# Token decays of a hybrid GLA and gated-delta block prepared inside its input projection, with the last gate stores on SP's queue

## The reference

```python
h = modulated_rmsnorm(x)                       # context and latent tokens, same weights
p = h @ w_in                                   # q, k, v, gates, a low rank r, and a, beta per head
log_alpha = -exp(a_log) * softplus(a + dt_bias)    # per token, direction and head
beta      = sigmoid(beta_b)
# gated delta rule, both directions, chunks of 64 tokens:
g = cumsum(log_alpha, over the chunk)
A = eye + tril(beta * (k @ k.T) * exp(g_i - g_j), -1)
U, W = solve(A, beta * v), solve(A, beta * exp(g) * k)
k_dec, a_chunk = k * exp(g_last - g), exp(g_last)
# beside it gated linear attention with a decay per key dimension
y = x + gate1 * (concat(norm(o) * silu(gate)) @ w_out)
out = rmsnorm(y + gate2 * (square(relu(modulated_rmsnorm(y) @ w1)) @ w2))
```

## Time and profile before

| | us |
|---|---|
| runs, median of 3 | 1803.25 (1802.39 to 1804.13) |
| profiled execution | 1795.54 |
| its span, first to last instruction | 1793.5 |
| PE busy in the span | 1572.9 |
| mean granted clock of PE | 0.951 of full |

### The profile page before, as it was taken

How to read it: one execution, slowest core, us unless ns; L and a number is a source line. 1 busy time by engine, 2 the same in 40 slices (tenths; PEclk the granted TensorE clock), 3 DMA queues, 4 the chain that set the end, 5 groups by cost and what they waited for, 6 DMA issues and landing times. The chain is left out here.

```text
span 1793.5 us, 35173 instructions
## 1 busy us (share of the span) xinstructions
PE 1572.9 (88%) x15022; PEld 1325.9 (74%) x15022; DVE 1011.8 (56%) x1542; ACT 641.6 (36%) x976; POOL 425.6 (24%) x376
## 2 busy tenths in 40 slices
PE   4599999999966888878776798789999989899997
PEld 1366887999966777777775587568888867787876
DVE  2534553101104776777776755845545588887975
ACT  3366435221102222232222223455545543333333
POOL 1301111111112455555554311323223200000000
PEclk7799999999987998999998899899999999999999
DMA  7213424426543543333322232034453487163422
GB/s 307 75 53 97 120 69 123 133 85 197 172 121 90 151 125 100 112 113 108 108 62 66 94 126 98 24 123 136 153 170 130 156 317 256 63 235 109 173 83 94
DMA packets 169565, 229.81 MB, mean 128 GB/s; under 512 B 34189, under 2 KB 101121, under 8 KB 168386
## 3 DMA queue, kind: packets, MB, share of 16 engines
q1 hardware_dynamic: 162562, 205.79, 35.2%
q0 software_dynamic: 6848, 21.76, 3.8%
HBM read 165.78 MB, written 61.73 MB: 127 GB/s over the span
## 5 line engine op out<-in xcount | busy, mean ns | idle before, releaser
L87 PE MATMUL fps<-xh_m,w1r_hi 128*128 128x512 f32 x448 | 177.6, 396 | 18.9 <-ACT s L2321 5.4
L87 PE MATMUL fps<-bh,ah 128*128 128x512 f32 x448 | 176.4, 394 | 13.6 <-DVE acc L2636 9.1
L88 PE MATMUL fps<-xl_m,w1r_hi 128*128 128x512 f32 x448 | 176.7, 394 | 0.0
L89 PE MATMUL fps<-xh_m,w1r_lo 128*128 128x512 f32 x448 | 176.5, 394 | 0.0
L89 PE MATMUL fps<-bh,al 128*128 128x512 f32 x448 | 176.0, 393 | 0.0
L88 PE MATMUL fps<-bl,ah 128*128 128x512 f32 x448 | 175.8, 392 | 0.0
L80 PE MATMUL ps_main<-hhi,whi 128*128 128x512 f32 (+3 forms) x360 | 136.4, 379 | 15.7 <-DVE wlo L647 11.8
L82 PE MATMUL ps_main<-hhi,wlo 128*128 128x512 f32 (+3 forms) x360 | 132.8, 369 | 0.0
L81 PE MATMUL ps_main<-hlo,whi 128*128 128x512 f32 (+3 forms) x360 | 132.7, 369 | 0.0
L2283 ACT ACTIVATE ah<-araw 128x2048 fp32r<-128x2048 f32 x28 | 53.7, 1918 | 186.4 <-PE fps L89 120.7
L80 PE MATMUL ps_main<-whi,hhi 128*128 128x256 f32 x416 | 120.0, 288 | 0.0
(11 more groups left out here) (307 smaller groups left out, 3596.6 us busy)
## 6 DMA issues: line engine op xcount, KB each, us to landing
s_hid<-hb SPq DMA_DIRECT2D x112, 256.0 KB, 2.3
araw<-s_hid SPq DMA_DIRECT2D x28, 1024.0 KB, 6.6
w1raw<-in_w_ff SPq DMA_DIRECT2D x16, 1024.0 KB, 6.2
w2b<-in_w_ff SPq DMA_DIRECT2D x16, 1024.0 KB, 6.2
raw<-in_w_in SPq DMA_DIRECT2D x14, 1024.0 KB, 5.2
wa<-in_w_ada SPq DMA_DIRECT2D x8, 1024.0 KB, 10.5
z_sb<-in_w_ada SPq DMA_DIRECT2D x16, 512.0 KB, 4.5
n_sb<-in_w_ada SPq DMA_DIRECT2D x16, 512.0 KB, 4.3
```

The source lines that it names most:

```text
L87: pe.matmul(out, lhi, rhi, start=start, stop=False, skip_group_check=True)
L88: pe.matmul(out, lhi, rlo, start=False, stop=False, skip_group_check=True)
L89: return pe.matmul(out, llo, rhi, start=False, stop=stop, skip_group_check=True)
```

## The change

Running sums, exponentials, token scales and turned rows are made inside the two value units of the projection. Their three masks are loaded there, into a buffer that the low-rank decays have left (`lr_x`). POOL stores the rows to DRAM during the second value unit. Results live in the memory of `K.gt2`, which is now allocated from the start; its own row gates are made at the start of merging. In mixing, SP issues the keys and `decays(0)` first; the remaining four masks follow, each with its own wait where it is used, instead of one wait for all. The stores of the last gate unit are issued by SP instead of POOL.

The core of the diff:

```diff
@@ project_phase, SP
+            def load_sums():
+                for b in range(2):
+                    sp.wait_ge(st_lr[b], 80)
+                for x, n in enumerate(("k_tri", "k_trix", "k_chunk")):
+                    sp.dma_start(sum_m[:, x], A[n]).then_inc(ld_sums, 16)
+            def store_gate(t):
+                sp.wait_ge(main_out, out_by[(LAST_GATE, "gate", t)])
+                nt = NSTORES - TL + t
+                sp.dma_start(S["gate"][t, :, 3 * W:4 * W], t_sb[:, nt % 4]).then_inc(st_g[t % 4], 16)
             for u in range(NU):
                 load_unit(u)
+                if u == VA - 1:
+                    load_sums()
...
             for g in range(10, NLATE):
                 load_late(g)
+                if g - 4 >= NLATE - TL:
+                    store_gate(g - 4 - NLATE + TL)
+            for t in range(TL - 4, TL):
+                store_gate(t)
+            for i in range(4):
+                sp.wait_ge(st_g[i], 32)
@@ project_phase, POOL
+                        if u == LAST_GATE:
+                            continue
+                        if (u, t) == (VA + 1, 6):
+                            pool.wait_ge(row_out, 1)
+                            pool.dma_start(S["row"].rearrange("x r n -> r x n"),
+                                           rowt.rearrange("r (x n) -> r x n", x=3)).then_inc(st_row, 16)
@@ project_phase, ACT: copy and exponentials after tile 3 of the first value unit, rows after tile 3 of the second
+                    if (u, j) == (VA, 3):
+                        act.wait_ge(g_ready, 1)
+                        act.activation(K.gcol, sums(0), ACT.Copy).then_inc(sm_act, 1)
+                        act.activation(K.sm[:, :, :, 2], sums(1), ACT.Exp).then_inc(sm_act, 1)
+                        act.activation(K.egc, sums(0), ACT.Exp).then_inc(sm_act, 1)
+                        act.activation(K.aB.rearrange("p c d t h -> p (c d t h)"), ps_tr[:, 0, 160:320], ACT.Exp).then_inc(sm_act, 1)
+                    if (u, j) == (VA + 1, 3):
+                        act.wait_ge(row_ready, 1)
+                        act.activation(rowt, ps_tr[:80, 1, :3 * P], ACT.Copy).then_inc(row_out, 1)
@@ project_phase, DVE: token_scales() at tile 6 of the first value unit, the 24 operations of lines 1271 to 1281
@@ project_phase, PE
+            def running_sums():
+                pe.wait_ge(ld_sums, 48)
+                pe.wait_ge(ab_kept, 2)
+                pe.wait_ge(tr_out, NTR * 8)
...              (the six products of lines 1453 and 1455)
+            def turn_rows():
+                pe.wait_ge(sm_act, 4)
...              (the three transposes of line 1469)
+                    if (u, j) == (VA, 0):
+                        running_sums()
+                    if (u, j) == (VA + 1, 0):
+                        turn_rows()
@@ mix_phase, SP
-            for dst, n in ((tri, "k_tri"), (trix, "k_trix"), (chunk, "k_chunk"), (lev_m, "k_lev"), (inc_m, "k_inc"),
-                           (eye, "k_eye"), (smask, "k_smask")):
-                sp.dma_start(dst[:], A[n]).then_inc(ld_mask, 16)
             keys(0)
+            decays(0)
+            constants(ld_lev, (lev_m, "k_lev"), (eye, "k_eye"))
+            constants(ld_tri, (tri, "k_tri"))
             linear(0)
             values(0)
             token_keys(0)
-            sp.wait_ge(rt_out, 1)
-            sp.dma_start(S["row"].rearrange("x r n -> r x n"), rowt[:]).then_inc(st_row, 16)
-            sp.wait_ge(st_row, 16)
-            decays(0)
+            constants(ld_inc, (inc_m, "k_inc"))
+            constants(ld_sel, (smask, "k_smask"))
@@ mix_phase, POOL
-            pool.wait_ge(ld_mask, 16 * N_MASK)
-            pool.wait_ge(sm_dve, 3)
             differ(0)
@@ mix_phase, ACT
+            act.preload_act_table_set("natural_log_exp_and_others")
-            for x in range(4):
+            for x in range(2):
@@ mix_phase, waits added in every step (DVE first_inverse and accumulate, PE first_inverse and cumulate)
+                dve.wait_ge(ld_lev, 32)
+                dve.wait_ge(ld_sel, 16)
+                    pe.wait_ge(ld_lev, 32)
+                pe.wait_ge(ld_tri, 16)
@@ mix_phase, PE: rows(2), rows(3), the sums and the turns are gone
@@ merge_phase, ACT and PE
+            for x in range(2):
+                act.wait_ge(rows_done, x + 1)
+                act.activation(K.gt2[:, x * 512:(x + 1) * 512], ps_p[:, x], ACT.Copy).then_inc(row_out, 1)
+            for x in range(2):
+                for i in range(4):
+                    last = pe.matmul(ps_p[:, x, i * P:(i + 1) * P], K.mod[:, 40 + 4 * x + i, 0:1].broadcast_to([P, P]), K.ident[:],
+                                     start=True, stop=True)
+                last.then_inc(rows_done, 1)
             inter(0)
```

More of the change, by code:

```diff
@@ L362, in project_phase @@
         ar_ready, ar_out, sel_done = m.sem("ar_ready"), m.sem("ar_out"), m.sem("sel_done")
+        ld_sums, ab_kept, g_ready = m.sem("ld_sums"), m.sem("ab_kept"), m.sem("pg_ready")
+        sm_act, sm_dve, row_ready, row_out, st_row = (
+            m.sem("psm_act"), m.sem("psm_dve"), m.sem("row_ready"), m.sem("row_out"), m.sem("st_row"))
+        st_g = [m.sem(f"st_g{i}") for i in range(4)]
+        VA = [un[0] for un in UNITS].index("va")
+        LAST_GATE = NU - 1
+        sum_m = lr_x[:].rearrange("p a n -> p (a n)")[:, :6 * P].rearrange("p (x d n) -> p x d n", x=3, d=2)
+        rowt = lr_e[:80, :3 * P]
         outs = []
@@ L623, in _ @@
                 else:
-                    if nt >= 4:
+                    if u == LAST_GATE and j >= 4:
+                        act.wait_ge(st_g[j % 4], 16)
+                    elif nt >= 4:
                         act.wait_ge(st_t[nt % 4], 16 * (nt // 4))
@@ L726, in _, with token_scales @@
             for t in range(NT):
-                dve.tensor_copy(K.beta[:, :, pos_of(t), :], zc[:, t, :].rearrange("p (z h) -> p z h", z=2))
+                last = dve.tensor_copy(K.beta[:, :, pos_of(t), :], zc[:, t, :].rearrange("p (z h) -> p z h", z=2))
+            last.then_inc(ab_kept, 1)
+            def token_scales():
+                half = lambda c: slice(c * C, (c + 1) * C)
+                dve.wait_ge(ab_kept, 2)
+                dve.wait_ge(sm_act, 4)
+                dve.tensor_copy(K.sm[:, :, :, 1], K.beta[:]).then_inc(sm_dve, 1)
+                dve.scalar_tensor_tensor(K.sm[:, :, :, 0], K.egc, -1.0, K.beta[:], ALU.mult, ALU.mult).then_inc(sm_dve, 1)
+                dve.wait_ge(sm_dve, 2)
+                for n in range(2):
+                    dve.tensor_copy(K.smn[half(n), n], K.sm[half(n), 0])
+                    for s in range(NT):
+                        back = 11 - s if s >= TC else 1 - s
+                        dve.tensor_copy(K.smn[half(1 - n), n, s], K.sm[half(1 - n), 1, back])
             for i, (u, kind, j, s) in enumerate(outs):
@@ L1529, in predict @@
                     after(pe, st_done[d], 2 * s + n)
-                if s == 0 and n == 0:
-                    pe.wait_ge(row_out, 4)
                 for h in range(NH):
@@ L1539, in query @@
                 pe.wait_ge(qd_done, s - TC + 1)
+                if s == TC and n == 0:
+                    pe.wait_ge(row_out, 2)
                 for d in R2:
@@ L2813, in hybrid_block @@
         K.beta = m.sb("beta", [P, 2, NT, NH])
+        K.gt2 = m.sb("gt2", [P, D])
+        K.sm, K.smn = (K.gt2[:, 240 * x:240 * (x + 1)].rearrange("p (d t z h) -> p d t z h", d=2, t=NT, z=3) for x in range(2))
+        K.gcol, K.egc = (K.gt2[:, 480 + 80 * x:560 + 80 * x].rearrange("p (d t h) -> p d t h", d=2, t=NT) for x in range(2))
+        K.aB = K.gt2[:, 640:800].rearrange("p (c d t h) -> p c d t h", c=2, d=2, t=NT)
         with ExitStack() as ctx_h:
```

94 lines of the change are left out of this document (33 added, 61 removed).

## The result

The kernel with the change took 1783.03 us, the median of 4 runs from 1780.32 to 1786.23, against 1802.99 us for the kernel before run beside it (4 runs, 1802.39 to 1804.13). The ratio is 0.9889 with a 95% interval of 0.9871 to 0.9908: faster by 16.6 to 23.3 us, with 20.0 in the middle. The forecast was -18.0 us, 1785.3. In four later series of runs the kernel before took 1795.2 to 1799.8 us at the median, so some of these 20 us may be chance; the repeat further down gives 16.4.

What follows compares the result with a forecast made beforehand. PE bounds the value units, a chain of waits the time from 523 to 559 us. Terms -5.3 - 15.2 + 2.0 + 0.5 + 0 = -18.0 us take 1803.25 to 1785.3, range 1780.5 to 1792.5.

Steps and rivals of the forecast that it cites:

- Stores on SP: End of projection: SP issues the last gate unit's stores, POOL's 5.045 us drain is hidden, release 523.4 not 528.7; gain 5.3 us.
- The rule of the Trainium skill that was weighed: Projection's end: issuing from another engine saves only issue time, about 0.28 us; the total would be -13.0 instead of -18.0.
- Prologue: Start of mixing: POOL's first product 8.3 us after the phase begins instead of 23.5; gain 15.2 us, keys' delay taken as nothing.
- `gla`: Mixing's start: decay operand could be late, ready at 15.4 against an inverse due at 14.1; taken as nothing, up to 1.3 lost.
- PE waiting for `gla`: Sign of being wrong: at mixing's start PE stands waiting for the decay operand's load.
- Value units: Projection's value units: PE takes up six products and three turned columns; loss 2.0 us, between 1.6 and 3.3.
- The four changes between kinds of matmul: PE in the projection's value units: one more instruction's 0.11 us for each change, an estimate.
- Added waits: Every mixing step: DVE gets 10 + 32 more semaphore waits, PE 20 + 10; loss 0.5 us, between 0 and 2.4.
- Gate rows: Start of merging: sixteen matmuls moved there while PE idles; taken as nothing, between a loss of 0.6 and a gain of 1.3.
- the longer head: Rival, mixing's start: keys and decay operand cost 1.5 and 1.3 us, waits 2.4; -13.3, 1790.0 us; chance 0.12.
- The drain stayed: Rival, projection's end: POOL's 5 us settle only when the phase ends, gain 0.3 instead of 5.3; 1790.3 us; chance 0.11.
- the last stage's clock: Rival: PE gets a lower clock after shorter rest; under about 0.945 eats 18 us, at 0.93 gives 1813; chance 0.03.

## Why the prediction was right, point by point

*Stores on SP.* Forecast -5.3, between 4.9 and 5.6; measured -5.6 in the trace. The drain fell under the last gate unit, and SP's own, forecast at the 0.37 us of the earlier trace rows, took 7 ns. That the drain "is paid on POOL's list whenever it comes" is shown by the run in which it was paid 27 us late. That it belongs to the stores that POOL issued fits its 50 to 54 ns for each transfer. The rule of the Trainium skill that was weighed (DMA: Bandwidth & Descriptors, section Issuing engines are not separate DMA queues) would have left this part at 0.3 us; here the trace does not agree, with 5.6 us, as the issuing engine also decides whose list, and whose drain, comes last. What stays open is why stores on SP alone gained nothing in the timings.

*Prologue.* Forecast a head of 8.3 us instead of 23.49; measured 8.19 and 8.41. The keys ahead of the spreading loads cost what the sum held for them and no more: with the order turned the head is 7.35, shorter by 0.85 us, which is their issue.

*`gla`.* This step failed, and "PE waiting for `gla`" was one of the signs of being wrong that I had named. I took nothing, as "Its queue is much emptier than in the row", with 1.3 us as the bound. It landed 5.8 us after its issue at 534.70, as in the earlier trace rows, and cost 1.60 us against before; in the other profiles 0.3 to 1.1 (6.08 to 6.90 less 5.81). Its queue was not emptier: by the sizes of SP's issues ahead of it some 1.6 MB stood there in both kernels, as the eight small loads (512 KB) took the place of masks. The bound had the right working and was 0.3 us too low; choosing its good end had no row behind it.

*Value units.* Forecast +2.0, measured +1.65. The sums came to 1.34 against 1.26 and the turns to 0.31 against 0.37. The four changes between kinds of matmul, put at 0.11 each, were not there.

*Added waits.* Forecast +0.5, measured 0.0: a step takes 42.48 before and 42.49 after at the same clock. A wait that is met when the engine comes to it costs nothing visible here, and the good end of the range would have been right. I had also named as a sign of being wrong a stretch from 580 to 976 us longer by more than 2.4. The eleven steps were 7.1 us longer in this pair of profiles, but the kernel before ran them as long (424.70 us) when profiled again.

*Gate rows.* Forecast 0, measured 0.0 in 134.64 against 134.72 us. The reason was incomplete, and the zero partly luck. I weighed a late start against a higher clock on PE alone, and looked for no effect on DVE and POOL. The first products gained 1.3 us by the clock, and the next group came 3.6 us later behind the collision; yet merging was as long in both kernels, and no run here shows why. The two profiles of 132.3 and 132.5 us go beyond the gain of 1.3 in my bound.

*The sum.* The forecast made -18.0; the landmarks -5.6 + 0.1 - 15.3 + 1.6 + 1.65 = -17.5; the timings -20.0 (16.6 to 23.3), and -16.4 (9.9 to 22.8) when repeated. A miss of 1.6 us (`gla`) and those of 0.5 (waits), 0.35 (value units) and 0.3 (stores) the other way hid in the total, so that it came out so close is partly luck. Of the rivals, the `gla` part of the longer head came true. The drain stayed nowhere; the last stage's clock stayed at 0.97.

## What to carry to other kernels

A phase boundary can carry a price of several us on one engine's list, so look in the trace for the list whose drain ends last and let that list end early, behind another engine's work. After a prologue has been emptied, the loads themselves are the critical path: order them by who needs them first, and cost each late one by the landing that the trace shows, not by how empty the queue ought to be. And where DVE and POOL both work in SBUF, a change of half a microsecond in when they meet went with two at the end of merging, which can't be planned from these rows.

## What the runs showed of the hardware that I had not expected

- POOL's drain at the end of the projection took 4392 to 5621 ns with 88 to 105 transfers issued, 60 to 85 ns more for each, and 4477 both at once and after 27 us of rest. At the end of merging, where it issues none, it took 2502 ns and covered a product of 2.41 us. SP's took 7 ns when it had issued the last stores, 370 when it had not.
- Eight 64 KB loads issued on two queues were all there 9.31 us after the first load, and on one queue 8.20, both times with the keys on SP's queue and `tri` and `gla` on ACT's.
- A DVE product of 0.34 us took 2.43 us when it began after a POOL instruction of 2.35 us, and ended 0.15 us after it.
- Identical mixing steps took 42.5 us at a granted clock of 1.00 and 47.4 at 0.86, and such dips came at other steps in every profile. That alone moves a single profile of this kernel by 9 us.
